# Second mixer: packed 64x64 chunk matrices in place of 128x128 ones, with the next pair's stages inside the levels

## The reference, cut to what matters

```python
def frame_step(state, inp):            # scanned over the 512 tokens; z = -kk, b = kk * a
    r_t, w_t, k_t, v_t, z_t, b_t = inp
    sz = jnp.einsum('bhij,bhj->bhi', state, z_t)
    state = (state * w_t[:, :, None, :]
             + sz[..., None] * b_t[:, :, None, :]
             + v_t[..., None] * k_t[:, :, None, :])
    y_t = jnp.einsum('bhij,bhj->bhi', state, r_t)
    return state, y_t
```

## Time and profile before

| | us |
|---|---|
| median of three runs | 3886.76 |
| the profiled execution | 3881.54 |
| its span, first to last instruction | 3879.9 |
| mean granted clock of TensorE | 0.962 |
| TensorE busy | 3639.5 |
| VectorE busy | 1987.4 |
| ScalarE busy | 1131.7 |
| GpSimd busy | 266.5 |

### The profile page before, as it was taken

One profiled execution on the slowest core, in us unless ns is written; L12 is line 12 of the kernel. 1 busy time (PEld: TensorE's weight loads), 2 busy tenths in 40 slices (PEclk: granted clock), 3 DMA queues, 4 the chain that ended last, 5 costly groups with the idle time before them and its releaser, 6 DMA issues. The chain is left out here.

```text
span 3879.9 us, 42339 instructions
## 1 busy us (share of the span) xinstructions
PE 3639.5 (94%) x16912; PEld 2860.0 (74%) x16918; DVE 1987.4 (51%) x2518; ACT 1131.7 (29%) x1458; POOL 266.5 (7%) x189
## 2 busy tenths in 40 slices
PE   7999999999999999769969999999999989999998
PEld 6887686688868886548846888675688866667887
DVE  5666545522352237985555223589522347964233
ACT  2222424322232223122223222334422233352222
POOL 0000000000000004700000000122000003300000
PEclk8999999999999999868969999999999999999999
DMA  5554220222222222200002222211122222102222
GB/s 224 185 194 152 79 98 33 76 94 94 94 76 97 98 98 75 76 1 1 1 3 74 97 98 97 76 66 55 39 103 97 98 87 76 66 31 80 96 97 76
DMA packets 47218, 325.62 MB, mean 84 GB/s; under 512 B 5232, under 2 KB 5488, under 8 KB 8688
## 3 DMA queue, kind: packets, MB, share of 16 engines
q1 hardware_dynamic: 41792, 290.10, 20.7%
q0 software_dynamic: 5296, 33.69, 2.4%
HBM read 321.67 MB, written 2.10 MB: 83 GB/s over the span
## 5 line engine op out<-in xcount | busy, mean ns | idle before, releaser
L1788 PE MATMUL PS<-HH,WH 128*128 128x512 f32 x2968 | 1171.8, 395 | 56.6 <-DVE HL L2136 43.4
L1789 PE MATMUL PS<-HL,WH 128*128 128x512 f32 x2968 | 1162.9, 392 | 0.0
L1790 PE MATMUL PS<-HH,WL 128*128 128x512 f32 x2968 | 1162.5, 392 | 0.0
L2118 DVE TENSOR_TENSOR WL<-RAW,WH 128x2048 fp32r<-128x2048 f32 x264 | 617.9, 2341 | 419.5 <-ACT WH L1991 413.0
L1788 PEld LDWEIGHTS PS<-HH,WH 128*128 128x128 f32 x2968 | 562.0, 189 | 199.6 <-issue 61.5
L1790 PEld LDWEIGHTS PS<-HH,WL 128*128 128x128 f32 x2968 | 561.8, 189 | 118.6
L1789 PEld LDWEIGHTS PS<-HL,WH 128*128 128x128 f32 x2968 | 562.3, 189 | 114.8 <-issue 0.2
L1991 ACT ACTIVATE WH<-RAW 128x2048 fp32r<-128x2048 f32 x264 | 503.7, 1908 | 355.8 <-PE PS L1790 348.3
L2160 DVE TENSOR_TENSOR A<-SG,PS 128x512 f32 (+1 forms) x132 | 90.8, 688 | 774.7 <-ACT SG L2034 774.6
L1788 PE MATMUL PS<-AH,WH 128*128 128x512 f32 x1056 | 411.8, 390 | 0.3 <-DVE CV L2245 0.3
L1789 PE MATMUL PS<-AL,WH 128*128 128x512 f32 x1056 | 411.5, 390 | 0.0
(11 more groups left out here) (367 smaller groups left out, 3624.7 us busy)
## 6 DMA issues: line engine op xcount, KB each, us to landing
RAW<-in_w SPq DMA_DIRECT2D x264, 1024.0 KB, 4.8
E<-in_ada POOLq DMA_DIRECT2D x28, 1024.0 KB, 5.1
E<-in_ada SPq DMA_DIRECT2D x4, 1024.0 KB, 11.4
G<-in_ada SPq DMA_DIRECT2D x4, 1024.0 KB, 19.5
X<-in_x SPq DMA_DIRECT2D x1, 2048.0 KB, 13.4
out_x<-A SPq DMA_DIRECT2D x8, 256.0 KB, 2.1
G<-in_cos POOLq DMA_DIRECT2D x4, 256.0 KB, 3.6
G<-in_sin POOLq DMA_DIRECT2D x4, 256.0 KB, 3.7
```

Source lines behind the costliest of these rows:

```text
L1788: nc.tensor.matmul(out, wh, xh, start=start, stop=False)
L1789: nc.tensor.matmul(out, wh, xl, start=False, stop=False)
L1790: return nc.tensor.matmul(out, wl, xh, start=False, stop=stop)
L2118: nc.vector.tensor_tensor(WL[:, w % 2, :], RAW[:, w % 2, :], WH[:, w % 2, :].bitcast(F32), ALU.subtract).then_inc(w_lo, 1)
```

## The change

All chunk matrices are kept as the 64-column halves that are not zero. Chunk c of tile n lies on partitions 64c to 64c + 63, so one AU2 of a pair holds [128, 2 heads, 16 tiles, 64], half the old size, and there are two of them, for even and odd pairs. TI2, XS2 and ML2 are packed the same way; ML2 is three buffers, by level modulo 3. The masks (`later`, `levels`) are 64 columns wide; an identity of 64 columns is packed behind `levels`.

Each product is now a 64x64 one in one quadrant of the array: the operands' partition half is its row half, the output's partition half its column half. In the levels the two chunks of a tile use the two diagonal quadrants in turn and write two partition halves of one bank. Chunk products, what the queries read, local values and merges go round all four quadrants, with one bank per row half. A copy, a mask or a sum in the levels covers both chunks at once and is 256 columns per head in place of 512.

Banks: 1 and 2 for x and the solved vectors, 3 and 4 for t (inverse in columns 0 to 255, its transpose in 256 to 511), 0, 5, 6 and 7 (`fill`) for the stages that stand inside the levels.

The order: between the x products and the t products of a level TensorE now runs another stage: in level 1 the queries and local values of pair m - 1, in level 2 the merges of pair m - 1, in level 3 the token transposes of pair m, in level 4 its value sums and the first half of pair m + 1's chunk products, in level 5 the second half. ScalarE's and VectorE's lists follow. `raise_` gets `landed`; with False the engine does not wait for its own instruction.

```diff
-        AU2 = A[:, 4:12, :]
-        TI2 = A[:, 12:16, :]
-        ML2, XS2, AV2, TZ2 = G[:, 4:6, :], G[:, 6:8, :], G[:, 12, :], G[:, 13:15, :]
+        AU2 = [A[:, n:n + 4, :].rearrange("p a s -> p (a s)").rearrange("p (r q t) -> p r q t", r=2, t=CH) for n in (4, 8)]
+        TI2 = A[:, 12:14, :].rearrange("p k (r q t) -> p k r q t", r=2, t=CH)
+        ML2 = [G[:, n, :].rearrange("p (r q t) -> p r q t", r=2, t=CH) for n in (4, 5, 7)]
+        XS2 = G[:, 6, :].rearrange("p (r q t) -> p r q t", r=2, t=CH)
+        BANK_X, BANK_T, BANK_F = (1, 2), (3, 4), (0, 5, 6, 7)
+        TOK_BANK = {3: 2, 2: 3, 0: 0, 1: 1}
...
-                if name != "pe":
+                if landed and name != "pe":
                     eng.wait_ge(step_sem[name], at[0])
...
-            pool.dma_start(LEVELS[:, 0:6 * P], T["levels"]).then_inc(m2_loads, 16)
+            pool.dma_start(LEVELS[:, 0:7 * CH], T["levels"]).then_inc(m2_loads, 16)
...
+        CHUNK_ROWS = [slice(0, 64), slice(64, P)]
...
+            def products(m, a):
+                if m:
+                    after("act", *(("av", m - 1) if a else ("tok", m - 1, 1)))
+                left, right = (B2, K2), (KK2, R2)[a]
+                for b in range(2):
+                    for n in range(NT):
+                        for c, to in enumerate(CHUNK_ROWS):
+                            tk = slice(n * P + c * CH, n * P + (c + 1) * CH)
+                            for par, ro in enumerate(CHUNK_ROWS):
+                                last = mm(tile(fill(2 * a + par)[to, :], 4 * b + n), left[b][ro, m, tk], right[ro, m, tk],
+                                          start=True, stop=True)
...
+            def x_products(m, l, par):
+                after("dve", "ml", m, l)
+                after("dve", *(("inv", m, l - 1, par) if l > 1 else ("t", m, 0, par)))
+                if l == 1 and m:
+                    after("act", "tz", m - 1, par)
                 for n in range(NT):
+                    for rows in CHUNK_ROWS:
+                        last = mm(tile(PS[BANK_X[par]][rows, :], n), ML2[l % 3][rows, par, n, :], TI2[rows, 0, par, n, :],
+                                  start=True, stop=True)
+                raise_(last, "x", m, l, par)
+            def t_products(m, l, par):
+                after("act", "x", m, l, par)
+                after("dve", *(("t", m, l - 1, par) if l > 1 else ("init", m)))
+                for kind in (0, 1) if l < 5 else (1,):
+                    for n in range(NT):
+                        for rows in CHUNK_ROWS:
+                            pair_ = XS2[rows, par, n, :], TI2[rows, 1, par, n, :]
+                            last = mm(tile(PS[BANK_T[par]][rows, :], 4 * kind + n), pair_[1 - kind], pair_[kind],
+                                      start=True, stop=True)
+                raise_(last, "t", m, l, par)
...
+            products(0, 0)
+            products(0, 1)
+            for m in range(4):
+                transposed(m, 0)
+                transposed(m, 1)
+                for l in range(1, 6):
+                    x_products(m, l, 0)
+                    x_products(m, l, 1)
+                    if l == 1 and m:
+                        read_queries(m - 1)
+                        local_values(m - 1)
+                    if l == 2 and m:
+                        merges(m - 1)
+                    if l == 3:
+                        if m == 0:
+                            after("dve", "au", 0, 1, 1)
+                        token_rows(m)
+                    if l == 4:
+                        value_sums(m)
+                    if l in (4, 5) and m < 3:
+                        products(m + 1, l - 4)
+                    t_products(m, l, 0)
+                    t_products(m, l, 1)
+                solved(m, 0)
+                solved(m, 1)
+            read_queries(3)
+            local_values(3)
+            merges(3)
...
+            for m in range(4):
+                level(m, 1)
                 for par in range(2):
                     after("pe", "t", m, 0, par)
+                    raise_(v.tensor_tensor(TI2[:, 0, par, :, :], ident.unsqueeze(1).to_broadcast([P, NT, CH]),
+                                           by_chunk(PS[BANK_T[par]][:, 0:4 * CH]), ALU.add), "t", m, 0, par, landed=False)
                 for l in range(1, 6):
+                    if l < 5:
+                        level(m, l + 1)
+                    if l == 1 and m:
+                        read_queries(m - 1)
+                    if l == 2:
+                        hat(m)
+                    elif last_taps:
+                        chain(tap(v, 3, last_taps.pop(0)))
                     for par in range(2):
                         after("pe", "t", m, l, par)
                         if l < 5:
+                            grow(0, par, "inv", m, l, par)
+                    for par in range(2):
+                        grow(1, par, "t", m, l, par)
+                    if l in (4, 5) and m < 3:
+                        for par in range(2):
+                            masked(m + 1, l - 4, par)
+                        if l == 4:
+                            level(m + 1, 0, landed=True)
+                if m < 3:
+                    after("pe", "tz", m, 1)
+                    start(m + 1)
+            read_queries(3)
```

More of the change, by code:

```diff
@@ L1201, in build_program @@
         dve_steps = [("kk raw",), ("sums",), ("kk v",), ("rk",), ("bonus read",), ("scaled",)]
+        PARS = (0, 1)
+        pe_steps += [("au", 0, a, par) for a in (0, 1) for par in PARS]
+        dve_steps += [("au", 0, 0, 0), ("au", 0, 0, 1), ("ml", 0, 0), ("init", 0), ("au", 0, 1, 0), ("au", 0, 1, 1)]
         for m_ in range(4):
-            pe_steps += [("tok", m_, x) for x in range(4)] + [("au", m_, n, par) for n in range(NT) for par in range(2)]
-            pe_steps += [("av", m_)]
-            act_steps += [("tok", m_, x) for x in range(4)] + [("av", m_)]
@@ L1206, in build_program @@
[L1206 to L1216, removed]
@@ L1220, in build_program @@
+            pe_steps += [("tz", m_, par) for par in PARS]
+            act_steps += [("tz", m_, par) for par in PARS]
+            dve_steps += [("init", m_ + 1)] if m_ < 3 else []
+        pe_steps += [("r", 3), ("yl", 3), ("mg", 3)]
+        act_steps += [("yl", 3), ("mg", 3)]
+        dve_steps += [("r", 3)]
         pe_steps += [("h", c) for c in range(NC2 - 1)] + [("y", m) for m in range(4)]
@@ L1316, in pe_mix2 @@
             after("dve", "scaled")
-            for m in range(4):
-                pair_products(pe, m, raise_, after)
+            pe_pairs(pe, raise_, after)
             for c in range(NC2 - 1):
@@ new lines, in level, with start @@
+            def level(m, l, landed=False):
+                mask = LEVELS[:, l * CH:(l + 1) * CH].unsqueeze(1).unsqueeze(1).to_broadcast([P, 2, NT, CH])
+                raise_(v.tensor_tensor(ML2[l % 3], AU2[m % 2][:, :, 0:NT, :], mask, ALU.mult), "ml", m, l, landed=landed)
+            ident = LEVELS[:, 6 * CH:7 * CH]
+            def start(m):
+                raise_(v.tensor_tensor(TI2[:, 1, :, :, :], ident.unsqueeze(1).unsqueeze(1).to_broadcast([P, 2, NT, CH]), ML2[0],
+                                       ALU.add), "init", m, landed=False)
@@ new lines, in grow, with read_queries @@
+            def grow(kind, par, *key):
+                to = TI2[:, kind, par, :, :]
+                raise_(v.tensor_tensor(to, to, by_chunk(PS[BANK_T[par]][:, 256 * kind:256 * kind + 256]), ALU.add), *key, landed=False)
+            def read_queries(m):
+                after("pe", "r", m)
+                for c in range(2):
+                    to = R2[:, m, :].rearrange("p (n c t) -> p n c t", c=2, t=CH)[:, :, c, :]
+                    last = v.tensor_tensor(to, to, by_chunk(fill(c)[:, 0:4 * CH]), ALU.add)
+                raise_(last, "r", m, landed=False)
@@ L1638, in dve_mix2 @@
                 for l in range(1, 6):
-                    for par in range(2):
-                        if l < 5:
-                            after("pe", "x", m, l, par)
-                            level(l + 1, par)
+                    if l < 5:
+                        level(m, l + 1)
+                    if l == 1 and m:
+                        read_queries(m - 1)
[3 more added lines that the diff above has]
+                        chain(tap(v, 3, last_taps.pop(0)))
```

283 lines of the change are left out of this document (148 added, 135 removed).

## The result

The changed kernel takes 3774.76 us (median of 4 runs, 3772.42 to 3776.22) against 3886.71 us for the kernel before (4 runs): a ratio of 0.9712, 95% interval 0.9695 to 0.9729, 112 us less. The profiled execution took 3772.42 us, its span is 3770.8. The time lies at the low end of the range, and the case that came true is not the likeliest one but the rival "full clock throughout" (3773).

The account below looks back on a forecast made before the run. TensorE was taken as the bound, in the four head pairs' 236.5 us stretch; 4 x 39 + 7 = 163 us there, 73.5 less, gave 3813 us against a median of 3886.76, range 3770 to 3850.

Parts of the forecast that it names:

- full clock throughout: Rival for the four pairs: TensorE keeps full clock, 4 x 29 + 7 = 123 us, total 3773; chance 0.18.
- likeliest case: Four pairs with both clocks, half the records each: 4 x 39 + 7 = 163 us, total 3813; chance 0.45.
- The clock: TensorE in each pair: half clock until level 3, then full until pauses at the change of pairs; 39 us a pair.
- the transposes as what lifts it: Token transposes in level 3, the only full-width products left, were expected to bring the clock back to full.
- The diagonal quadrants: 576 records a pair alternating two diagonal quadrants, fully overlapped: 0.0583 / 2 us each, 16.8 us a pair at full clock.
- The rival that they don't overlap: Diagonal quadrants sharing a PSUM bank run one by one: 179 to 311 us for the pairs, 3829 to 3961; chance 0.10.
- Products round four quadrants: Chunk products, queries, local values, merges: 320 records a pair at 0.020 us, 6.4 us at full clock.
- The level chain: x, ScalarE copy, t, VectorE sums, next x: 3.1 us a level at full clock, plus whatever is emitted inside.
- 4 us of waits a pair: TensorE's pauses per pair at full clock, including 0.75 us before solved and 1.2 before the next x0.
- 7 us at start and end: Outside the pairs' steady state: about 3 us before pair 0 can run and about 4 behind the last solved product.
- Self-waits: Dropping engines' waits for their own instructions: nearly nothing, 0.03 us between VectorE instructions at most.
- Levels DMA and taps: Smaller levels DMA at the mixer's start, worth 0 to 1 us, taken as 0; moved taps, nearly nothing.

Follow-up runs that it names:

- the repeat: The changed kernel itself, unaltered, run again beside some of the follow-up runs: 3774.3 us, ratio 0.9713 against the kernel before.
- one-quadrant kernel: Changed kernel with only pair 0's chunk products reordered, all of one quadrant and then the next: 3782.87 us, one execution.
- long-runs kernel: Changed kernel with every stage of small products in the longest runs of one quadrant its loops allow: 3848.13 us, ratio 0.9901 against the kernel before.
- in-sequence kernel: Changed kernel's packed products in the old order, each pair finished before the next begins: 3786.01 us, ratio 0.9750 against the kernel before.
- the repeated products: Changed kernel with the first half of pair 1's chunk products computed nine times, 512 records more: 3785.67 us, one execution.
- rows-apart kernel: Changed kernel with the row-half loop outside the tile loop in transposed products, x, t, solved and value sums: 3789.64 us, ratio 0.9759 against the kernel before.

## Why the prediction was wrong in its likeliest case and right in a rival

**The clock, the step that failed.** The prediction took "half clock from the start of a pair to its level 3", 39 us a pair; measured is half clock for 5.5 us in pair 0 and full clock from there on, but for one fall of 3.4 us in the repeat. By its own sum that is 4 x 39 + 7 = 163 against 4 x 29 + 7 = 123, and 123.5 was measured. Neither reason for it held for this order of quadrants. That small tiles may not raise the clock was read from y of the earlier trace rows, which never got it back. The quadrants of that stage came in long runs of one row half, and so do the products of the one-quadrant kernel, which waited until 1718.0. Behind two diagonal quadrants in turn it was up by 1707.9. And the transposes as what lifts it: in the changed kernel the clock was up before the first of them. In the long-runs kernel the forecast's picture did come true: half clock from the start of pair 0 through 30.9 us of small tiles, full clock within the transposes of level 3. So the reading of the transposes was sound where nothing had raised the clock earlier, and what failed was that small tiles alone would not. The rule of the Trainium skill ("TensorE: Matmul & The Clock Gate", Part 4: PE-mode transpose) that transposes do not count for the clock decided nothing for the changed kernel; the rise at 1737.2 of the long-runs kernel, with only transposes running since 1735.03, speaks against it, in one profile, as did the rise behind 3.6 us of transposes in the earlier trace rows. That the pauses at the change of pairs let the clock fall, with half of every pair lost by it, was wrong as well: it fell at none of the three changes in one profile and at one of them in the other, and was back 3.4 us later; so it was behind the pauses of 3 us of the in-sequence kernel.

**The diagonal quadrants**, taken as fully side by side (0.0583 / 2), measured 0.029: right. The rival that they don't overlap, 0.10, would have given 0.058. The rule of the Trainium skill behind that rival ("TensorEngine Tiling (Array Packing)", Gotcha 1: PSUM Pressure), that different row tiles cannot access one PSUM bank at the same time, does not hold in this trace: x products and t products write the two partition halves of one bank side by side at 0.029 us a record.

**Products round four quadrants** were taken at 0.020, between 0.0146 and 0.0292. A short stage runs at the lower end: 0.0146 in the repeated products. Over 1280 records that is 7 us less than forecast.

**The level chain** was right: 3.1 us forecast and 3.1 measured in level 1 of pair 0, and what is emitted inside adds in full (level 4 of pair 0 lasts 5.0 us: 3.1, 32 records of value sums at 0.029 and 64 chunk-product records at 0.0147, 0.9 us each). 4 us of waits a pair: the two named are 7.4 / 4 = 1.9 a pair (forecast 0.75 + 1.2). All pauses of TensorE in the stage are 123.50 - 104.34 = 19.2 us, of which 6.4 are the stops; the other 12.8 stand against 16 + 7. The prediction had the old kernel's pause before a fall at 1.5 us; TensorE's timeline has 1.84, the clock turning inside it.

**The instruction supply** was no step at all. The change issues 3072 instructions more (45411 against 42339, by the two pages), and its stops cost 7.4 us. At 0.0146 us a record a block of 128 lasts 1.9 us, at 0.029 it lasts 3.7, at the old 0.116 it lasted 14.8. This miss and the four-quadrant pace have the same size and cancel, so that 123 for full clock came out so well is partly luck: TensorE is busy for 104.3 us where the sum had 4 x 25 = 100 (the first 5.5 us at half clock are in it), and its pauses are 19.2 where it had 23.

**7 us at start and end**: pair 0's own start went at half clock but the window of pair 0 is still 30.2 us; the last pair is 34.1, some 4 more than the others, as forecast. **Self-waits** were put at nearly nothing ("0.03 us between VectorE instructions at most"); they are worth about 5 us of stage, with VectorE busy for 82.8 us of it where it was 74.2. **Levels DMA and taps** at nothing: the stage begins at 1701.7 in place of 1701.8, and from the variances to the end it is 1898.2 us after and 1894.3 before, where nothing was changed; executions of the kernel before differ by more than these 4 us (3880.47 to 3889.13).

The range of 3770 to 3850 held 3774.76 only because it reached to this rival: the likeliest case, 3813, was 38 us off by the clock. The rival's own 0.18 was too little.

## What to carry to other kernels

Where a product fills a quarter of the array, give neighbouring instructions different quadrants: the order of issue alone was two thirds of the gain here (75 of 113 us), costs nothing, and gave 13 us in the merges and 11 in the states as single edits. With the same order the clock came up within 6 us here, where one quadrant at a time in pair 0's first products took 16 us and in all stages 33. And when records get below some 0.03 us, as in this stage, look for stops on "issue" with instruction packets beside them.

## What the runs showed of the hardware that was not expected

- Instruction supply: 16 KB for each 256 TensorE instructions, a stop of 1.1 to 1.9 us every 128 records of a stream at 0.0146 us a record, 0.028 sustained.
- A matmul of a free quadrant starts ahead of an older one that waits for its own quadrant. In the rows-apart kernel the program has all x products (L1435) before the merges (L1488); TensorE's timeline there:

```profile
1745.98 0.28 PE L1488 MATMUL PS<-A,G 64*64 64x64 f32 x3
1746.04 0.22 PE L1435 MATMUL PS<-A,G 64*64 64x64 f32 x1
1746.09 0.22 PE L1488 MATMUL PS<-A,G 64*64 64x64 f32 x1
1746.10 0.22 PE L1435 MATMUL PS<-A,G 64*64 64x64 f32 x1
```

  The Trainium skill ("TensorE: Matmul & The Clock Gate", Part 3: Packing small matmuls — row/col tiling) says that matmuls start and end strictly in order. These starts disagree; ends are modelled in the trace and say nothing. This lookahead is one reason why runs of eight records cost 16 us and not 80.
- Two VectorE instructions without a wait between them overlap: 72 of 0.418 us in 27.0 us.
- A fall of the clock can be short: 3.4 us in the in-sequence kernel and in the repeat of the changed one, where the old kernel lost it for 10.3 and the states behind never regained it before y had ended. Two executions of one program can differ in whether it falls.
- Runs of one quadrant kept the full clock for 163 us in the long-runs kernel but did not raise it in 30.9.
